# Gate and up by seven block products in place of eight, in a streaming encoder trunk on one core

## The reference

```
def half_ffn(x, i, n):
    h = 0.5 * swiglu(x, ffn_w1[i, n], ffn_w3[i, n], ffn_w2[i, n])      # (silu(x @ w1) * (x @ w3)) @ w2
    return layer_norm(ALPHA * x + h, ln_g[i, 2 * n], ln_b[i, 2 * n])
```

## Time and profile before

| | us |
|---|---|
| median of 3 runs | 2569.51 |
| lowest and highest run | 2569.48, 2569.84 |
| span of the profiled execution | 2569.5 |
| TensorE busy in it | 2544.0 (99%) |
| VectorE, ScalarE, GpSimd busy | 1107.3, 816.1, 142.8 |

### The profile page before, as it was taken

One profiled execution on the slowest core, in us unless ns is written; L12 is line 12 of the kernel. 1 busy time (PEld: TensorE's weight loads), 2 busy tenths in 40 slices (PEclk: granted clock), 3 DMA queues, 4 the chain that ended last, 5 costly groups with the idle time before them and its releaser, 6 DMA issues.

```text
span 2569.5 us, 37727 instructions
## 1 busy us (share of the span) xinstructions
PE 2544.0 (99%) x16284; PEld 2303.6 (90%) x16284; DVE 1107.3 (43%) x1477; ACT 816.1 (32%) x1272; POOL 142.8 (6%) x199
## 2 busy tenths in 40 slices
PE   8999999999999999999999999999999999999998
PEld 8998998899989988899899988777776999899987
DVE  4223323662233236733232261666666732233267
ACT  4222222132222223432122122666665322122133
POOL 3000000100000000000000001222123000000000
PEclk9999999899999999999999999999999999999999
DMA  6213222322132222332232124677776332232121
GB/s 182 73 62 95 72 73 70 107 79 72 62 95 73 71 78 74 96 85 79 62 96 69 62 74 135 192 219 199 218 212 192 97 93 67 62 99 75 53 95 66
DMA packets 376757, 259.09 MB, mean 101 GB/s; under 512 B 10449, under 2 KB 339153, under 8 KB 376592
## 3 DMA queue, kind: packets, MB, share of 16 engines
q1 hardware_dynamic: 371488, 239.64, 32.0%
q0 software_dynamic: 5104, 17.04, 2.0%
HBM read 248.22 MB, written 8.42 MB: 100 GB/s over the span
## 4 chain that ended last, share of the span: by engine, by line
PE 95%; DVE 2%; ACT 1%; issue 1%; DMA 1%; POOL 0%; SPq 0%; DVEq 0%; ACTq 0%
PE ps L1775 86%; PE ps L520 5%; PE ps L552 2%; PE ps L1871 1%; DMA raw<-in_ffn_w_dram 1%; PE ps L628 0%; ACT e_buf L1089 0%; ACT wt L1114 0%; DVE ring L1376 0%; ACT kc_t L1073 0%; DVE x L1420 0%; DVE s_sum L1539 0%; DVE x L1428 0%; DVE e_buf L1504 0%; PE ps L543 0%
## 5 line engine op out<-in xcount | busy, mean ns | idle before, releaser
L1775 PE MATMUL ps<-xt_hi,ring 128*128 128x256 f32 (+1 forms) x6160 | 1340.0, 309 | 4.0 <-ACT xt_hi L1050 2.3
L1775 PEld LDWEIGHTS ps<-xt_hi,ring 128*128 128x128 f32 x6160 | 1035.9, 190 | 12.7 <-issue 9.6
L1775 PE MATMUL ps<-xt_lo,ring 128*128 128x384 f32 (+1 forms) x3080 | 944.7, 309 | 0.0
L1775 PEld LDWEIGHTS ps<-xt_lo,ring 128*128 128x128 f32 x3080 | 583.8, 190 | 0.2
L1775 PE MATMUL ps<-ring,h_hi 128*128 128x512 f32 x1760 | 550.0, 392 | 0.0
L1030 ACT ACTIVATE ring<-raw 128x1024 fp32r<-128x1024 f32 x326 | 324.8, 1029 | 428.3 <-PE ps L1775 351.7
L1376 DVE TENSOR_TENSOR ring<-raw,ring 128x1024 fp32r<-128x1024 f32 x326 | 383.3, 1204 | 137.2 <-ACT ring L1030 132.8
L1775 PEld LDWEIGHTS ps<-ring,h_hi 128*128 128x128 f32 x1760 | 332.7, 189 | 68.9
L1638 DVE SCALAR_TENSOR_TENSOR act<-act,ps 128x384 f32<-128x384 f32 (+1 forms) x176 | 85.8, 488 | 667.3 <-PE ps L1775 667.3
L1775 PE MATMUL ps<-ring,h_lo 128*128 128x512 f32 x880 | 344.2, 391 | 0.0
L1264 ACT ACTIVATE h_hi<-act 128x384 fp32r<-128x384 f32 (+1 forms) x176 | 83.0, 472 | 626.4 <-DVE act L1638 626.4
(11 more groups left out here) (137 smaller groups left out, 1606.0 us busy)
## 6 DMA issues: line engine op xcount, KB each, us to landing
raw<-in_ffn_w_dram SPq DMA_DIRECT2D x256, 512.0 KB, 4.4
k_raw<-in_cache_k_dram SPq DMA_DIRECT2D x128, 256.0 KB, 4.8
v_raw<-in_cache_v_dram SPq DMA_DIRECT2D x128, 256.0 KB, 4.3
raw<-in_sb_w_in_dram SPq DMA_DIRECT2D x24, 512.0 KB, 5.8
raw<-in_ple_w_gate_dram SPq DMA_DIRECT2D x16, 512.0 KB, 4.7
g_b<-in_ln_g_dram POOLq DMA_DIRECT2D x8, 512.0 KB, 4.2
b_b<-in_ln_b_dram POOLq DMA_DIRECT2D x8, 512.0 KB, 5.9
raw<-in_ffn_w_dram SPq DMA_DIRECT2D x16, 256.0 KB, 3.4
```

Source lines behind the costliest of these rows:

```text
L1775: return pe.matmul(out, w, xx, start=first, stop=last, skip_group_check=True)
```

## The change

`gu` and `down` become one stage `ffn`. x^T is seen as 2 x 2 blocks (rows in two halves of 320, features in two halves of 512), and a pair's weights as 2 x 2 blocks (features in two halves; gate and up). Their product, eight block products, is formed from seven, by Winograd's scheme: of the weights the gate's first half, the up's second half and four differences are needed, of x four sums (S1 to S4) and three blocks. A block product is four chunks x three matmuls of 320 columns, so a pair takes 84 matmuls. Products that are added are accumulated in one bank; what two results share is copied out in between (`c1`, `c5`, `r_sum`).

- Weights: VectorE forms two differences of 512 columns in one instruction (`first_diffs`), GpSimd the other two (`diffs`); ring items per pair are A (gate, 1024 columns), B and D (differences, 1024 each) and C (half of up, 512), all converted to high and low.
- x: for each FFN GpSimd and VectorE form the sums (`quarter_of`, `pair_sums`, `pair_sums12`, `pair_sums43`), TensorE transposes them (`turn_sums12`, `turn_sums43`, `turn_x22`), ScalarE and VectorE divide them. An FFN's input takes 24 + 40 transposes where it took 40. The sample tile now comes first (`ORDER`).
- Inner chunks are kept for four pairs, not eleven. The down products are made in six rounds (of 2, 4, 4, 4, 4 and 4 chunks), each added to x: 660 matmuls as before, 60 additions where there were 20. Rounds 0 to 4 follow pairs 2, 6, 10, 14 and 18. In the last round the halves of the features alternate, so that a tile is complete after every second group.
- The bands of the pool mixer are built by GpSimd after the first FFN's pairs, and not at the start.

The core of it (the order of the engines in the steady part, the start of an FFN, and what a round adds):

```diff
+ROUNDS = ((0, 2), (2, 4), (6, 4), (10, 4), (14, 4), (18, 4))
+ROUND_AFTER = {first + n: r for r, (first, n) in enumerate(ROUNDS[:-1])}
...
@@ gpsimd @@
+            def diffs(st, q):
+
+                n = st.q0 + q
+                pool.wait_ge(t13_done, n + 1)
+                pool.tensor_tensor(t_buf[:, 1, :], raw_of(("up", st, q))[:, HK:], t_buf[:, 0, :],
+                                   ALU.subtract).then_inc(t24_done, 1)
...
+                if st.kind == "load":
+                    quarter_of(st)
+                    diffs(st.next, 0)
+                    pair_sums(st)
...
@@ scalar @@
+                first_product(st, 0)
+                cvt_to(unit["A", 1] + 1)
+                if prev.kind == "load":
+                    quarter_rounded(prev)
...
+                hi_sums43(prev, 1)
+                hi_x22(prev, 1)
+                cvt_to(unit["B", 1] + 1)
+                fifth_product(st, 0)
+                common_sum(st, 0)
+                cvt_to(unit["A", 2] + 1)
...
+                for q in range(3, FC):
+                    r = ROUND_AFTER.get(q, LAST if q == FC - 1 else None)
+                    cvt_to(unit["D", q] + 1)
+                    first_product(st, q)
+                    cvt_to(unit["A", q + 1] + 1 if r is None else unit["U", (r, 0)] + 1)
+                    if r is None:
+                        cvt_to(unit["C", q + 1] + 1)
+                    silu_of_first(st, q)
+                    cvt_to(unit["B", q + 1] + 1 if r is None else unit["U", (r, 1)] + 1)
+                    fifth_product(st, q)
+                    common_sum(st, q)
+                    if r is not None:
+                        cvt_to(unit["U", (r, 2)] + 1)
+                    silu_of_second(st, q - 1)
+                    hidden_hi(st, q - 1)
+                    if r is not None:
+                        cvt_to(unit["U", (r, 3)] + 1)
...
@@ vector @@
+                gate_of_first(st, 0)
+                low_sums12(prev, 0)
+                low_x22(prev, 0)
+                pair_sums12(prev)
+                low_sums43(prev, 0)
+                pair_sums43(prev)
+                low_sums12(prev, 1)
+                gate_of_first(st, 1)
+                cvt_to(unit["D", 0] + 3)
+                low_sums43(prev, 1)
+                low_x22(prev, 1)
+                first_diffs(st, 1)
+                cvt_to(unit["B", 1] + 1)
+                cvt_to(unit["C", 1] + 1)
+                hidden_of_first(st, 0)
+                cvt_to(unit["A", 2] + 1)
...
+                for q in range(3, FC):
+                    r = ROUND_AFTER.get(q, LAST if q == FC - 1 else None)
+                    if q - 1 not in ROUND_AFTER:
+                        hidden_lo(st, q - 2)
+                        hidden_of_first(st, q - 1)
+                    cvt_to(unit["D", q] + 1)
+                    if r is None:
+                        first_diffs(st, q + 1)
+                    gate_of_first(st, q)
+                    cvt_to(unit["A", q + 1] + 1 if r is None else unit["U", (r, 0)] + 1)
+                    up_of_second(st, q - 1)
+                    if r is None:
+                        cvt_to(unit["B", q + 1] + 1)
+                    else:
+                        cvt_to(unit["U", (r, 2)] + 1)
+                    hidden_of_second(st, q - 1)
+                    if r is not None:
+                        cvt_to(unit["U", (r, 3)] + 1)
+                    if r is not None and r < LAST:
+                        down_sums(st, r, q)
...
+            def down_sums(st, r, q):
+
+                unit = st.item
+                hidden_lo(st, q - 1)
+                hidden_of_first(st, q)
...
@@ tensor @@
+            def period(st, q):
+
+                product1(st, q)
+                product2(st, q)
+                product7(st, q - 1)
+                product5(st, q)
+                product6(st, q)
+                product4(st, q - 1)
+                product3(st, q)
...
+                        if n == 0:
+                            pe.wait_ge(h_lo_done, st.q0 + first + c + 1)
...
+                    product1(st, 0)
+                    turn_sums12(prev, 0)
+                    product2(st, 0)
+                    turn_x22(prev, 0)
+                    product1(st, 1)
+                    turn_sums43(prev, 0)
+                    turn_sums12(prev, 1)
+                    product2(st, 1)
+                    turn_sums43(prev, 1)
+                    turn_x22(prev, 1)
+                    product5(st, 0)
+                    product6(st, 0)
+                    product3(st, 0)
+                    product1(st, 2)
```

More of the change, by code:

```diff
@@ L162, in plan_stages, with add_pieces @@
-    part = y = gate = norm = piece = free = units = 0
+                stages.append(Stage("embed", layer, ln=3, then="none" if layer == DEPTH - 1 else "blocks"))
+    y = gate = norm = free = pieces = ffns = 0
+    on_bank = {}
+    def add_pieces(st, names):
+        nonlocal pieces
+        for name, bank in names:
+            pieces += 1
+            wide = 1 if name.startswith("X22") else 2
+            before = max(on_bank.get(b, 0) for b in range(bank, bank + wide))
+            for b in range(bank, bank + wide):
+                on_bank[b] = pieces
+            st.piece[name] = (pieces, bank, before)
@@ L163, in plan_stages @@
     for st, before in zip(stages, [None] + stages[:-1]):
-        st.part0, st.y0, st.gate0, st.norm0, st.free0, st.u0 = part, y, gate, norm, free, units
+        st.y0, st.gate0, st.norm0, st.free0 = y, gate, norm, free
         st.prev = before
-        if st.kind == "embed":
-            st.pt0 = piece
-            piece += PLE // P
-        st.piece0 = piece
-        if st.kind == "gu":
-            st.head = before.then != "none"
-            part += 2 * FH
-            units += 2 * FH
-        if st.kind in ("down", "out", "embed"):
+        if before is not None:
+            before.next = st
@@ new lines, in streaming_trunk @@
+        slot_free = {}
+        holders = {}
+        for u, item in enumerate(items):
+            waits = []
+            for col in range(item.col, item.col + item.cols, HK):
+                before = holders.get((item.slot, col))
+                if before is not None and freed[before] not in waits:
+                    waits.append(freed[before])
+                holders[item.slot, col] = u
+            if item.stage.kind == "out":
+                if item.slot == SLOT["c"] and item.at < 4:
+                    waits = [(z_full, NU * PAIRS)]
+                elif item.slot == SLOT["d"]:
+                    waits = [(s_full, NU * PAIRS - 2)]
+                elif item.slot in (SLOT["e"], SLOT["f"], SLOT["g"]):
+                    waits = [(pv_done, NU * PAIRS), (k_stored, 32 * PAIRS)]
+            slot_free[u] = waits
@@ new lines, in _ @@
+                    low(st, 0)
+                    low(st, 1)
+                    first_diffs(st.next, 0)
+                    cvt_to(1)
+                    low(st, 2)
+                    cvt_to(2)
+                if st.kind == "ffn":
+                    block_products(st)
+                    ahead = 2 if st.next.kind == "pool" else 4
+                    first = st.next.u0
+                    for j in range(TILES):
+                        evacuate_down(st, LAST, 2 * j)
+                        evacuate_down(st, LAST, 2 * j + 1)
+                        if j < 3:
+                            cvt_to(first + min(ahead, j + 1))
+                        normalise(st, j)
+                        if 1 <= j <= 3:
+                            low(st, j - 1)
+                        if j == 3:
+                            cvt_to(first + ahead)
@@ L1706, in _ @@
                     add_bias(TILES)
+                    if st.then == "blocks":
+                        first_diffs(st.next, 0)
                     for t in range(TILES):
@@ new lines, in block_product @@
+            def block_product(bank, u, col, x_hi, x_lo, first):
+                slot = items[u].slot
+                for c in range(HC):
+                    for hl, xx in ((0, x_hi), (0, x_lo), (1, x_hi)):
+                        ins = mm(ps[:, bank, 0:HT], ring[:, slot, hl, col + c * P:col + (c + 1) * P], xx[:, c, :],
+                                 first and c == 0 and hl == 0 and xx is x_hi, c == HC - 1 and hl == 1)
+                return ins
+            x11 = tuple(xx[:, 0:HC, 0:HT] for xx in (xt_hi, xt_lo))
```

1476 lines of the change are left out of this document (973 added, 503 removed).

## The result

The changed kernel takes 2574.7 us (median of 12 runs, 2570.3 to 2579.5), the kernel before in the same comparison 2569.2 (12 runs, 2567.2 to 2571.0): ratio 1.0022, 95% interval 1.0015 to 1.003. It is slower by 0.2%, 5.5 us, where 2549 and a gain were predicted. The range of 2480 to 2600 holds it, and so does the band of 2564 to 2575 that the prediction called no change, at its upper edge. The profiled execution has a span of 2572.9 us and a time of 2574.7, so the median agrees with it. Between the spans of the two profiled executions lie +3.4 us, where the sum said -20.8. In every run listed for the two kernels the time is 1.7 to 1.8 above the span, so that execution would have a time of some 2571.2 (an estimate), 2 us above its median.

What follows compares the result with a forecast made beforehand. TensorE, busy 99% of the span, was taken as the bound. Terms -154.9 + 9.5 + 28.8 + 11.2 + 5.2 + 10.4 + 65.6 + 3.4 = -20.8 took 2569.5 to 2549 us; 8-in-10 range 2480 to 2600.

Steps and rivals of the forecast that it cites:

- The matmuls: Gate and up products: 84 matmuls of 320 columns a pair at 0.1467 us, -154.9 us; extra transposes +9.5.
- Where a round follows: Down rounds: TensorE waits 1.8 us for VectorE's low part of h, +28.8; round 0 and pair 1 +11.2; last pair +5.2.
- The last round: Last down round: VectorE needs 8 us per tile against TensorE's 5.46, so three turns wait 2.6 us in all: +10.4.
- The starts: Starts of the four FFNs: TensorE waits for c5, low parts, sums and weights; 24.3, 16.9, 14.0 and 10.4, together +65.6 us.
- The clock: Longest new waits may drop TensorE's clock again, at 1.7 us each; bounds 0 and four times, two taken: +3.4 us.
- The prediction's own alarm: Sign in the profile after: the forecast is wrong if the clock is below 0.97 over the span.
- The clock falls at the rounds too: Rival, chance 0.12: twenty waits of some 2 us at the rounds each cost 1.7 of clock, giving 2583 us.
- The waits are shorter: Rival, chance 0.25: ScalarE and VectorE overlap more, covering the rounds' and half of the starts' own waits, giving 2489 us.
- VectorE becomes the bound: Rival, chance 0.14: in plain periods GpSimd's differences hold VectorE's port, 11.7 of 12.3 us filled; at 13.5 a period, 2635 us.
- my 3.2 us of cover: Plain period: VectorE is busy 9.1 of 12.3 us, so TensorE loses nothing beyond its matmuls; the rest is cover.

Runs made afterwards that it cites:

- experiment 3: Changed kernel with VectorE taking the low part of h ahead of each down round's fourth weight unit (second in round 0): 2535.5 us.
- experiment 8: Changed kernel with VectorE taking the low part of weights A and B twice from each FFN's fifth pair on: 2638.4 us.
- fill_again: Changed kernel with unread 384-column matmuls put into TensorE's waits at the FFN starts, fills no longer than their waits: 2568.6 us.

## Why the prediction was wrong

**The matmuls: right.** 320 columns take 0.1467 us, 84 of them 12.32; the midpoint of 256 and 384 columns was the value. With the transposes -144.1 against -145.4. (The 143.6 that the prediction set beside it is 143.4: 88 x 1.63.)

**Where a round follows: right in place and mechanism.** +28.8, +11.2 and +5.2 are 45.2 for the low part of h and up_of_second. The trace has 34.1 + 3.6 of idle time and 6.3 of refills, 44.0; moving the step gave 39 us back (experiment 3). A wait of rounds 1 to 4 is 1.47 and not 1.8; the refill of 0.26, which I had not counted, makes up for it.

**The last round: right in size.** I had 2.6 us each; in FFNs 2 to 4 TensorE waits 1.5 to 1.9 for a tile's norm, and has 1.2 of refills. In the first the wait is one of 3.4, at the first use of a tile in `pool`.

**The starts: sum near, parts off.** Behind the first product I had 18.7, 11.8, 14.0 and 10.4 us; the account has 18.5, 11.2, 14.5 and 8.6. Ahead of it I had 5.6, 5.1, 0 and 0, and the trace shows 4.3, 4.8, 4.9 and 3.9, the distance from the last down matmul to the first product against before. `embed` and `out` were not untouched: in `embed` the first tile's turn waits 3.7 us for its norm where it waited 1.2, and 1.6 us are clock. Together 70.7 against 65.6. The figure behind `pool` is too kind: it is taken to 531.20, where the kernel before begins its second product, and its first, in parts, was already done by then (from 524.34). Counted as idle time and refills alone, the four stretches ahead of the first product lost 4.2, 6.9, 3.3 and 3.8, 18.2 in all, so the sum of the starts stands. The prediction's reading of the earlier trace rows has the same flaw: the matmuls from 519.24 on are those of `pool` (256 columns, from the ring), and the parts begin at 524.34. TensorE idled only 1.5 of those 22.3 us, and not 7.1.

**The clock: this is the step that failed,** a term of +3.4 us that measured +22.7 in the account. "The longest new waits (4 us, then 2.5 behind one product) may do so again. Bounds 0 and four times; I take two, **+3.4**." The price of 1.7 came from a single drop behind a single wait, and I let only the longest waits bring one. The trace has this, over the first sums' wait:

```profile
11.90:35.80 23.90, 9.24 (x36) 8.80 (x37) 5.18 (x6) 4.90 (x9) 10.92 (x10) 0.50 0.18 53
```

Between the first two waits lies one product, 12 matmuls in 3.2 us in place of 1.76; the clock stays at 0.50, 1.2 GHz, until 35.8, with 14.7 of 23.9 us idle. A mean clock of 0.981 over 2572.9 us stands for some 0.019 x 2 x 2572.9 = 98 us at the lower level, 0.995 before for 26. It came at the starts and in `pool`, at every start more than once, and made the matmuls 22.7 us longer than before. `pool` itself had three slow stretches before the change too; what is new lies in the main at the four starts, whose windows (clock 0.78, 0.88, 0.83 and 0.92) hold 57 of the 98 us. The Trainium skill, "TensorE: Matmul & The Clock Gate", section "HAM oscillation — how this bites in real kernels", describes this shape: short bursts of matmuls between waits, each met again by the lower clock. The trace agrees with it (0.50 over the 23.9 us above), and I had not priced a stretch as a whole. Filling the waits took 13.9 of the 36.3 away and gave 10.4 back in the profiled execution, 6.1 in the median. So the missing 19.3 are in the trace, but not all of them would come back with the clock: part of a slow product is covered by what TensorE would have waited for anyway. By the 10.4 of 13.9 some 14 of them would (an estimate), and the rest would stand as longer waits; that the waits came out within 3.6 us is in this part luck. The prediction's own alarm, a clock below 0.97, did not go off at 0.981: it was set too low to catch a miss of 20 us.

**The rivals.** "The clock falls at the rounds too" had the right engine and the wrong place: over rounds the windows show 1.00. "The waits are shorter" fell. "VectorE becomes the bound" did not come true, but it was nearer than my 3.2 us of cover said: 9.94 us of 12.32 are busy, and experiment 8 shows that 2.6 more cost 1.5 a period. The chances of 0.67, 0.08 and 0.25 rested on a sum with one term at less than a sixth of its size; a forecast that is 20 us from no change, with some 120 us of new waits in it, should have given more to the other side. By the prediction's own bands the result is "no change", which had 0.08.

## What to carry over

Where an optimization takes work from the busiest engine and adds steps on the others, count its new waits at the starts and ends of stages separately, and price each with three things: the idle time, some 0.25 us of refill, and for a cluster of waits the matmuls of the whole stretch at the lower clock, as an upper bound (here some three quarters of it was time). Then read the written order of each in-order queue at those waits: here moves of a few instructions, none of which removes work, turned +0.2% into -2.6%. A spare engine's cover is the time in hand at each wait, not its idle time in a period.

## What was not expected of the hardware

Two engines slowed each other in every plain period. From VectorE's and GpSimd's timelines of the changed kernel:

```profile
187.33 1.22 DVE L1807 TENSOR_TENSOR ring<-t_buf,ring 128x1024 fp32r<-128x1024 f32 x1
...
190.23 2.14 DVE L1807 TENSOR_TENSOR ring<-raw,ring 128x1024 fp32r<-128x1024 f32 x1
192.30 0.48 DVE L1997 TENSOR_TENSOR tmp<-ps,tmp 128x320 f32<-128x320 f32 x1
192.70 1.38 DVE L1807 TENSOR_TENSOR ring<-raw,ring 128x512 fp32r<-128x512 f32 x1
```

```profile
189.99 1.30 POOL L1111 TENSOR_TENSOR t_buf<-raw,t_buf 128x512 f32<-128x512 f32 x1 [9.57 <-DVE t_buf L1820]
191.37 2.16 POOL L1114 TENSOR_TENSOR t_buf<-raw,t_buf 128x512 f32<-128x512 f32 x1
```

The same conversion of 1024 takes 1.22 us alone and 2.14 beside GpSimd's difference, the one of 512 takes 1.38 in place of 0.68, and the difference 2.16 in place of 1.30. It is so in 56 of the 88 pairs, the plain ones. Each is longer by about what is left of the other engine's instruction when it starts (191.29 - 190.23 = 1.06, 192.37 - 191.37 = 1.00, 193.53 - 192.70 = 0.83), so in these rows the two take turns rather than run together. That is 1.6 us of VectorE in a period, hidden in each plain period here. How the clock's part divides between the waits of a start, and why the clock of a run goes with its time in fill_again and not in the changed kernel, is not settled by these runs.
